# The low-rank gate's panel ahead of the last pair of heads, and its logits inside that pair's last panel

## What is computed

```
q, k, v, qg, kg, vg, glr, rg = split(h @ w_in)          # glr is [T, 16]
o_a = moba_attention(q, k, v, rp_table)                 # 8 heads of 64, here in 4 pairs
log_a = log_sigmoid(glr @ w_gate_up + b_gate) / 16      # the logits
o_g = gla_chunked(qg, kg, vg, log_a)
o_g = rms_norm(o_g, g_norm) * silu(rg)
x = x + concat([o_a, o_g]) @ w_out
```

## Time and profile before

| | us |
| --- | --- |
| median of 3 executions | 1539.41 |
| lowest and highest | 1537.49, 1540.6 |
| the profiled execution | 1537.66 |
| its span, first to last instruction | 1535.9 |
| TensorE busy (98% of the span) | 1502.2 |
| VectorE busy | 881.2 |
| ScalarE busy | 562.6 |

### The profile page before, as it was taken

One profiled execution on the slowest core, in us unless ns is written; L12 is line 12 of the kernel. 1 busy time (PEld: TensorE's weight loads), 2 busy tenths in 40 slices (PEclk: granted clock), 3 DMA queues, 4 the chain that ended last, 5 costly groups with the idle time before them and its releaser, 6 DMA issues.

```text
span 1535.9 us, 20560 instructions
## 1 busy us (share of the span) xinstructions
PE 1502.2 (98%) x7096; PEld 1229.1 (80%) x7096; DVE 881.2 (57%) x1420; ACT 562.6 (37%) x827; POOL 24.4 (2%) x20
## 2 busy tenths in 40 slices
PE   7999999999999999999999999899999999999996
PEld 6877778788888888888888877788888888888885
DVE  6736664675655655434448778955665652255432
ACT  5214544324433333333226545434443321123220
POOL 0000000000000000000000000000000000000000
PEclk9999999999999999999999999999999999999998
DMA  6523222223322222232332231312122322222211
GB/s 238 209 84 96 75 75 89 91 74 105 110 96 96 96 96 96 97 108 96 124 110 83 98 122 55 110 65 73 63 76 83 109 96 93 88 98 99 90 66 55
DMA packets 43014, 148.95 MB, mean 97 GB/s; under 512 B 4632, under 2 KB 5032, under 8 KB 42836
## 3 DMA queue, kind: packets, MB, share of 16 engines
q1 hardware_dynamic: 38688, 137.38, 26.3%
q10 hardware_dynamic: 4276, 10.89, 2.1%
HBM read 146.13 MB, written 6.06 MB: 99 GB/s over the span
## 4 chain that ended last, share of the span: by engine, by line
PE 71%; issue 24%; DVE 4%; ACT 0%; DMA 0%; POOLq 0%; POOL 0%; DVEq 0%; ACTq 0%
PE ps L1078 23%; PE ps L1080 22%; PE ps L1079 22%; PE ps L1208 1%; PE ps L1221 1%; DVE wl L691 1%; DVE a L1843 1%; DVE qe L1830 1%; PE ps L1118 0%; DMA x<-x_dram 0%; PE ps L2182 0%; DVE x L2029 0%; PE ps L1111 0%; DVE msum L1641 0%; DVE hl L703 0%
## 5 line engine op out<-in xcount | busy, mean ns | idle before, releaser
L478 ACT ACTIVATE wh<-stage 128x1024 fp32r<-128x1024 f32 x255 | 270.1, 1059 | 564.2 <-PE ps L1080 563.1
L1078 PE MATMUL ps<-hh,wh 128*128 128x512 f32 x1096 | 436.4, 398 | 10.8 <-DVE hl L703 10.8
L1080 PE MATMUL ps<-hh,wl 128*128 128x512 f32 x1096 | 428.5, 391 | 0.0
L1079 PE MATMUL ps<-hl,wh 128*128 128x512 f32 x1096 | 428.0, 390 | 0.0
L691 DVE TENSOR_TENSOR wl<-stage,wh 128x1024 fp32r<-128x1024 f32 x255 | 311.9, 1224 | 192.8 <-ACT wh L478 192.5
L1078 PEld LDWEIGHTS ps<-hh,wh 128*128 128x128 f32 x1096 | 206.4, 188 | 59.8 <-issue 14.6
L1080 PEld LDWEIGHTS ps<-hh,wl 128*128 128x128 f32 x1096 | 206.3, 188 | 43.7
L1079 PEld LDWEIGHTS ps<-hl,wh 128*128 128x128 f32 x1096 | 206.6, 189 | 39.7
L1080 PE MATMUL ps<-ah,wl 128*128 128x512 f32 x432 | 170.8, 395 | 0.0
L1079 PE MATMUL ps<-al,wh 128*128 128x512 f32 x432 | 170.7, 395 | 0.0
L1078 PE MATMUL ps<-ah,wh 128*128 128x512 f32 x432 | 170.7, 395 | 0.0
(11 more groups left out here) (307 smaller groups left out, 1825.3 us busy)
## 6 DMA issues: line engine op xcount, KB each, us to landing
stage<-stream_dram SPq DMA_DIRECT2D x255, 512.0 KB, 3.2
bias_lines<-bias_line ACTq DMA_DIRECT2D x1, 3840.0 KB
x<-x_dram ACTq DMA_DIRECT2D x4, 512.0 KB, 9.7
bias<-bias_lines ACTq DMA_DIRECT2D x4, 512.0 KB, 5.0
out_dram<-x SPq DMA_DIRECT2D x8, 256.0 KB, 2.1
bias<-bias_lines ACTq DMA_DIRECT2D x4, 256.0 KB, 2.9
mem<-mem_dram ACTq DMA_DIRECT2D x1, 1024.0 KB, 4.8
early<-early_dram SPq DMA_DIRECT2D x1, 512.0 KB, 12.1
```

Of the source, the lines that this page charges most:

```text
L478: A(b.wh[:, p.slot, :], b.stage[:, p.slot, :], ACT.Copy).then_inc(s.hi_ready, 1)
L1078: MM(out, wh, xh, start=start, stop=False, skip_group_check=True)
L1079: MM(out, wh, xl, start=False, stop=False, skip_group_check=True)
L1080: return MM(out, wl, xh, start=False, stop=stop, skip_group_check=True)
```

## The change

The low-rank panel is taken out from behind the last pair and put ahead of it. In the stream of panels it comes between the third and the fourth pair; the last pair's panels are now numbered from P_LAST. Each engine's program follows: TensorE calls `features(Panel(P_GLR), ...)` before `pair_body(3, True)`, VectorE copies its result at the head of the last pair. The two logits' products are made by a new step `logits(r)` inside the last pair's last panel, ahead of its tiles 2 and 6, and go to the banks 4 and 5 instead of 6 and 7. `glr` and `wgu` now lie in `diag` (so rows name them `diag`), and `wgu` is loaded by ScalarE ahead of the pair loop. The three copies of weights and subtractions at the pair's end keep their places and carry other names.

```diff
@@ scalar_program
     pair_parts(0)
+    act.dma_start(b.wgu[0:16, :], dram["wgu"]).then_inc(s.wgu_in, 16)
     hi(Panel(P_VA2 + 3 + RING))
...
     act.dma_start(b.masks[:], dram["late"].rearrange("p (l q) -> p l q", q=P)).then_inc(s.late_in, 16)
-    act.dma_start(b.wgu[0:16, :], dram["wgu"]).then_inc(s.late_in, 16)
-    hi(Panel(P_GLR + RING))
+    hi(Panel(P_LAST + 3 + RING))
     for r in range(2):
         act.wait_ge(s.logit_done, r + 1)
-        A(b.la[:, r, :], b.ps[:, 6 + r, :], ACT.Abs, bias=col(b, "b_gate2", r)).then_inc(s.logit_abs, 1)
+        A(b.la[:, r, :], b.ps[:, 4 + r, :], ACT.Abs, bias=col(b, "b_gate2", r)).then_inc(s.logit_abs, 1)
@@ vector_program, pair_body
+        if last:
+            evac_row(Panel(P_GLR), 0, b.glr, E_GLR % 4)
         dve.wait_ge(s.bias_in, 16 * i + 80)
...
         evac(3)
         if last:
-            lo(Panel(P_PAIRS + 3 + RING, RING, i))
+            lo(Panel(P_LAST + 2 + RING))
@@ behind the pairs
-    dve.wait_ge(s.evac, E_PAIRS + 16)
+    dve.wait_ge(s.evac, E_LAST + 4)
     V.tensor_scalar(b.zg[:, 0:2, :], b.zg[:, 0:2, :], 0.125, None, ALU.mult).then_inc(s.q_scaled, 1)
...
-    evac_row(Panel(P_GLR), 0, b.glr[:], E_GLR % 4)
-    lo(Panel(P_GLR + RING))
+    lo(Panel(P_LAST + 3 + RING))
@@ block2_tensor
+    def logits(r):
+        pe.wait_ge(s.wgu_in, 16)
+        pe.wait_ge(s.evac, E_GLR + 1)
+        if r == 0:
+            pe.wait_ge(s.o_evac, 11)
+        else:
+            pe.wait_ge(s.turned_ready, 48)
+        MM(b.ps[:, 4 + r, :], b.wgu[0:16, P * r:P * r + P], b.glr[0:16, :], start=True,
+           stop=True).then_inc(s.logit_done, 1)
...
+                   {0: [tn(1, 3)], 2: [lambda: logits(0)], 4: [second_values], 6: [lambda: logits(1)]} if last else
                    {0: [tn(1, 3)], 4: [second_values]})
...
     with pe.Fori(0, 3) as i:
         pair_body(i)
-    pair_body(3)
     features(Panel(P_GLR), E_GLR, E_GLR % 4)
-    pe.wait_ge(s.late_in, 32)
-    pe.wait_ge(s.evac, E_GLR + 1)
-    pe.wait_ge(s.turned_ready, 48)
-    pe.wait_ge(s.o_evac, 12)
-    for r in range(2):
-        MM(b.ps[:, 6 + r, :], b.wgu[0:16, P * r:P * r + P], b.glr[0:16, :], start=True,
-           stop=True).then_inc(s.logit_done, 1)
+    pair_body(3, True)
     tokens(P_VG, E_VG, s.v_done)
```

More of the change, by code:

```diff
@@ L48 @@
 P_END1 = P_DOWN + 3 * KT
-(P_QA, P_KA, P_VA2, P_PAIRS, P_GLR, P_VG, P_XV, P_WOUT2, P_XQ, P_XO, P_UP_A, P_DOWN_A, P_UP_B, P_DOWN_B,
- P_END) = (P_END1 + n for n in (0, 4, 8, 12, 28, 29, 33, 41, 49, 57, 65, 81, 97, 113, 129))
+(P_QA, P_KA, P_VA2, P_PAIRS, P_GLR, P_LAST, P_VG, P_XV, P_WOUT2, P_XQ, P_XO, P_UP_A, P_DOWN_A, P_UP_B, P_DOWN_B,
+ P_END) = (P_END1 + n for n in (0, 4, 8, 12, 24, 25, 29, 33, 41, 49, 57, 65, 81, 97, 113, 129))
 E_U, E_VA, E_POOL, E_Q, E_K, E_V, E_GATE, E_PROJ, E_WOUT, E_UP, E_DOWN = 0, 2, 4, 6, 10, 14, 18, 42, 66, 74, 118
 E_END1 = E_DOWN + KT
-(E_QA, E_KA, E_VA2, E_PAIRS, E_GLR, E_VG, E_XV, E_WOUT2, E_XQ, E_XO, E_UP_A, E_DOWN_A, E_UP_B, E_DOWN_B,
- E_END) = (E_END1 + n for n in (0, 4, 8, 12, 28, 29, 33, 37, 45, 53, 61, 77, 85, 101, 109))
+(E_QA, E_KA, E_VA2, E_PAIRS, E_GLR, E_LAST, E_VG, E_XV, E_WOUT2, E_XQ, E_XO, E_UP_A, E_DOWN_A, E_UP_B, E_DOWN_B,
+ E_END) = (E_END1 + n for n in (0, 4, 8, 12, 24, 25, 29, 33, 37, 45, 53, 61, 77, 85, 101, 109))
 M = 256
@@ L220, in semaphores @@
     s.a_cleared, s.ke_cleared, s.q_scaled, s.qk_product = named("a_cleared ke_cleared q_scaled qk_product")
+    (s.wgu_in,) = named("wgu_in")
     (s.xk_hi, s.xk_ready, s.xv_hi, s.xv_ready) = named(
@@ L370, in place @@
     b.vx = at("vx", R(44), [MT, D])
-    b.glr = at("glr", R(52), [T])
-    b.wgu = at("wgu", R(54), [256])
+    b.glr = b.diag[:, 0, :]
+    b.wgu = b.diag[:, 1, 0:256]
     b.yh2 = at("yh2", R(68), [KT, T], F32R)
@@ L1410, in pair_body @@
         act.wait_ge(s.silued, i + 1)
-        act.wait_ge(s.evac, 4 * i + E_PAIRS + 2)
+        act.wait_ge(s.evac, E_LAST + 2 if last else 4 * i + E_PAIRS + 2)
         AR(b.tmp[:, 0, :], b.rg[:, i, :], ACT.Tanh, scale=0.5).then_inc(s.gated, 1)
@@ L1685, in evac @@
         def evac(u):
-            p = Panel(P_PAIRS + u, RING, i)
-            slot = (E_PAIRS + u) % 4
+            p = Panel(P_LAST + u) if last else Panel(P_PAIRS + u, RING, i)
+            slot = ((E_LAST if last else E_PAIRS) + u) % 4
             if u == 0:
@@ L1721, in pair_body @@
         dve.wait_ge(s.gated, i + 25)
-        dve.wait_ge(s.evac, 4 * i + E_PAIRS + 2)
+        dve.wait_ge(s.evac, E_LAST + 2 if last else 4 * i + E_PAIRS + 2)
         V.scalar_tensor_tensor(b.rg[:, i, :], b.tmp[:, 0, :], 1.0, b.rg[:, i, :], ALU.add,
@@ L1744, in block2_vector @@
     st.mark(V.memset(b.reset[:, 0::CHUNK], 0.0))
-    evac_row(Panel(P_GLR), 0, b.glr[:], E_GLR % 4)
-    lo(Panel(P_GLR + RING))
+    lo(Panel(P_LAST + 3 + RING))
     for r in range(2):
         dve.wait_ge(s.logit_abs, r + 1)
-        st.mark(V.tensor_scalar(b.b[:, r, :], b.ps[:, 6 + r, :], col(b, "b_gate2", r), 0.0, ALU.add, ALU.min))
+        st.mark(V.tensor_scalar(b.b[:, r, :], b.ps[:, 4 + r, :], col(b, "b_gate2", r), 0.0, ALU.add, ALU.min))
     q = b.zg[:, 0:2, :].rearrange("p r t -> p (r t)")
@@ L1790, in block2_vector @@
         step()
-    dve.wait_ge(s.late_in, 32)
+    dve.wait_ge(s.late_in, 16)
     dve.wait_ge(s.a_cleared, 2)
@@ L2064, in block2_tensor, with pair_body @@
     pe.wait_ge(s.rowa_ready, 1)
-    def pair_body(i):
+    def logits(r):
[7 more added lines that the diff above has]
+           stop=True).then_inc(s.logit_done, 1)
+    def pair_body(i, last=False):
         def sc(n):
@@ L2096, in pair_body @@
             moving = {} if u < 2 else {"xh": b.memh, "xl": b.meml, "width": M}
-            features(Panel(P_PAIRS + u, RING, i), E_PAIRS + u + RING * i, (E_PAIRS + u) % 4,
-                     between=between[u], **moving)
+            p = Panel(P_LAST + u) if last else Panel(P_PAIRS + u, RING, i)
+            e = E_LAST + u if last else E_PAIRS + u + RING * i
+            features(p, e, (E_LAST + u if last else E_PAIRS + u) % 4, between=between[u], **moving)
     with pe.Fori(0, 3) as i:
         pair_body(i)
-    pair_body(3)
     features(Panel(P_GLR), E_GLR, E_GLR % 4)
-    pe.wait_ge(s.late_in, 32)
-    pe.wait_ge(s.evac, E_GLR + 1)
-    pe.wait_ge(s.turned_ready, 48)
-    pe.wait_ge(s.o_evac, 12)
-    for r in range(2):
-        MM(b.ps[:, 6 + r, :], b.wgu[0:16, P * r:P * r + P], b.glr[0:16, :], start=True,
-           stop=True).then_inc(s.logit_done, 1)
+    pair_body(3, True)
     tokens(P_VG, E_VG, s.v_done)
@@ L2365, in layout @@
     half = FF2 // 2
-    stream += [chunk_panels(w2[:, 0:1024]), row_panels(w2[:, 1024:1536]), pairs, glr,
+    stream += [chunk_panels(w2[:, 0:1024]), row_panels(w2[:, 1024:1536]), pairs[:12], glr, pairs[12:],
                row_panels(w2[:, 2048:2560]), row_panels(xkv[:, D:D + 512]), row_panels(xkv[:, D + 512:2 * D]), chunk_panels(a["w_out_2"][0]),
```

## The result

| | before | changed |
| --- | --- | --- |
| median of 20 executions each, us | 1539.26 | 1541.66 |
| lowest and highest | 1536.01, 1542.52 | 1540.14, 1544.99 |
| ratio of the two (95% interval) | | 1.0017 (1.0011 to 1.0024) |
| profiled execution, its span | 1537.66, 1535.9 | 1540.36, 1538.6 |

The changed kernel is slower by 2.40 us, 0.17%. The interval of the ratio lies wholly above 1, so the difference is clear of the noise.

What follows compares the result with a forecast made beforehand. TensorE, busy 1502.2 of 1535.9 us, was taken as the bound, with VectorE deciding at L2118: -0.77 on TensorE plus 3.2 of standing gave +2.45, so 1540.1 profiled or 1541.9 against the median; range 1538.6 to 1544.3.

Steps and rivals of the forecast that it cites:

- The copy of `glr` leaves the path, hidden at the head of the last pair.: At the old join behind the last pair: the copy's 0.99 us leaves TensorE's path; VectorE's 0.69 for it is covered.
- 1.05 for each insertion, TensorE 0.77 sooner.: Last pair's last panel: two inserted products cost 2.10 us against the join's 2.87, so `vg` starts 0.77 sooner, at 918.11.
- VectorE starts 6.53 later and waits 0.53 for the panel.: VectorE's chain from the last head's values starts at 915.79; its `kx` copy waits 0.53 us for the pair's last panel.
- Net +3.2 at the running sums.: End of VectorE's running sums: delays less removed waits and the copy shift it by +3.2 us, to 933.85.
- 9.42 from the sums to q*k.: VectorE from the running sums' end to the q*k product: 9.64 less a wait of 0.22, done at 943.27.
- TensorE stands for 3.2.: Ahead of the `ones` products (L2118): TensorE, done at 940.13, waits 3.2 us for VectorE's q*k, where before it waited for nothing.
- +2.45 at L2118 and carried 1 to 1.: The `ones` products start at 943.35 instead of 940.90, +2.45 us, and everything behind carries this to the end.
- The gain is kept: Rival: VectorE's chain to q*k is done in time, TensorE does not stand ahead of L2118; 1538.6 us, chance 0.10.
- the point of decision: For the kept gain: q*k must end before 940.13 + 0.1, for which 3.2 us have to leave VectorE's chain.
- The products are dear: Rival: each logits' product inside the panel pays a further break like the join's 0.99; +4.4, 1543.8 us, chance 0.10.
- The clock falls: Rival: the granted clock falls behind TensorE's stand at L2118, costing 1.4 us more; +3.9, 1543.3 us, chance 0.35.

Runs made afterwards that it cites:

- e5: Changed kernel with both logits' products back behind the last pair and the scalings of x spread 3, 2, 3 along VectorE's chain; 1536.98 us, ratio 0.9983.
- e3: Changed kernel with the eight scalings of x moved from ahead of the running sums to behind the chain's three steps; 1537.9 us, ratio 0.999.
- e1: Changed kernel with both logits' products back behind the last pair, the low-rank panel staying ahead of it; 1537.9 us, ratio 0.9994.
- e4: Changed kernel with each logits' product made twice in a row into the same bank; profiled span 1540.4 us.
- e8: Changed kernel with both logits' products together ahead of tile 6 of the last pair's last panel; profiled span 1539.9 us.
- r1: Changed kernel unedited, profiled again on another chip to see its granted clock; 1540.96 us.
- r2: Changed kernel unedited, second repeat on another chip to see its granted clock; 1541.38 us.
- r3: Changed kernel unedited, third repeat on another chip to see its granted clock; 1542.99 us.
- e6: Kernel before, with scalings spread, two level differences and their exponentials made early, a third difference and a subtraction ahead of the states; 1536.64 us, ratio 0.9981.

## Why the prediction was right

The forecast against its own reference was 1537.66 + 2.45 = 1540.1 for a profiled execution; it was 1540.36, of which 0.25 is older than the change. Against the median it was 1541.9; it is 1541.66. That the mechanism held is shown below; that the median agrees to 0.2 us is in part luck, since the forecast had the clock stay up behind the wait, and in three of four profiles of this kernel it did not. Step by step, with the marks taken out:

- **The copy of `glr` leaves the path, hidden at the head of the last pair.** Right. In e5, where VectorE is not late, TensorE is 0.88 earlier for it.
- **1.05 for each insertion, TensorE 0.77 sooner.** The mechanism held, the term was too small. The first product stands between 912.09 and 913.35: 913.35 - 912.21 = 1.14, and the matmul behind it is followed after 0.22 instead of 0.12, another 0.10: 1.24. The row of L1152 had been read up to the next matmul's start and without what that one costs, 0.11 more there; the remaining 0.08 is not explained. Two cost 2.48, not 2.10, against 2.87 for the join: `vg` starts 0.39 sooner (918.49 in before's time, forecast 918.11). In e3 the saving at `ones` is 0.56; 0.11 more is the first `vg` matmul, which no longer follows a plain fp32 product.
- **VectorE starts 6.53 later and waits 0.53 for the panel.** The start is 916.22 - 0.25 = 915.97, forecast 915.79: the first product's 0.19. The wait is 0.76; of the 0.23 above the forecast 0.19 is the second product's. e1 and e4 show that these two terms are real: 1.94 come back with the products behind the pair, 1.71 are added with two more.
- **Net +3.2 at the running sums.** They end at 934.16 - 0.25 = 933.91, forecast 933.85. `kx` starts 0.38 later than forecast (918.94 - 0.25 against 918.31). That is offset because steps in a row overlap at more places than the two I counted: from `kx` to the sums' end it takes 15.22, where the sum had 15.54.
- **9.42 from the sums to q*k.** 943.47 - 934.16 = 9.31. q*k ends at 943.22 in before's time, forecast 943.27.
- **TensorE stands for 3.2.** From 940.51, when the next matmul could have been issued, to 943.52: 3.01. It came 0.13 later than forecast and was released 0.08 sooner.
- **+2.45 at L2118 and carried 1 to 1.** +2.37, and 48.82 against 48.78 in the stretch behind it.

**The rivals.** *The gain is kept* needed a shorter VectorE chain; e3 made it so, and the point of decision was as put: q*k done at 939.84, before TensorE arrives, and no wait. With the scalings where they are it was not to be had. *The products are dear* is refuted: 1.24, not 2.0. *The clock falls* came true in part. It did not in the profile on which the step-by-step reading rests; it did in three of the four profiles of this kernel, by 1.6 to 2.8 us in the stretch and not by the 1.4 that the rival took from the earlier trace rows. That can be more than the whole forecast difference of 2.45, yet the total is the forecast's. In the two of those three profiles that lose 2.8, 1.4 to 1.65 is missing from the loss at the second wait. The rest is in what the median of before contains: its profile (1537.66) is 1.6 below its own median, one step of the last column. So the clock's part of the difference of the medians came out near nothing: 2.40 measured, 2.37 of work. That it cancels here is a reading of thirteen profiles. The runs that were only timed have their mean granted clock on record, to a thousandth, and at the same clock the two kernels lie further apart: at 0.993 the changed kernel has 1541.66 (median of 7), before 1539.63 (12, beside e1 to e4) and 1539.11 (8, beside e5 to e8), 2.0 to 2.6 less; at 0.994 it is 3.7 to 4.0 and at 0.992 2.9 to 3.7, with three to eight executions a side. So the cancelling is rough at best. Had it not cancelled, the rival's 1543.3 would have been the better figure, and its chance should have been put above the forecast's own: the row for it was there, a fall behind 2.07.

The rule cited with this rival, from the Trainium skill, TensorE: Matmul & The Clock Gate, Part 1 (What's actually happening), that the low level is the default and activity releases it, would have the clock low behind the stand. Five profiles agree (0.50 at r1's 944.00), the first of the changed kernel does not (1.00 in the same window).

**What stays open.** What decides whether the clock falls behind the same wait in the same kernel; whether a fall at the first place makes one at the second less likely (it was absent in e4, r1 and r2, present in e8 and r3); and what makes a kernel's share of executions at the lower clock. That share is why the medians of e1 and e3, 1.6 below before, are lower than their starts of `ones` (+0.43 and -0.56) say: eight of e1's ten executions have a mean granted clock of 0.995 or 0.996, three of e3's ten, and two of the 25 of before. At the same clock the order is that of the starts. At 0.993 e3 is 0.7 below before (three against 12) and e1 1.7 above (two against 12); in the other group e5 is 0.7 below at 0.993 and 0.9 at 0.994 (its start of `ones`: -0.88), and e6 2.4 to 2.7 below at 0.992 to 0.994 (its stretch: -2.39).

## What to carry to other kernels

Work on one engine is also cover for what the others do beneath it. Before moving it, list that and ask whether it is late for anything behind; here 5.48 us of a low-rank panel covered the copy of `kx`, a subtraction, a scaling and the clears. An early product delays every chain that forks behind it by its whole time, so, while the other engine is the late one, a small product belongs behind the fork, beside another of its kind. And a difference of 2 us between two profiles is read from a mark ahead of the change to the point where the engines join again: total times here move by steps of 1.6 us with the clock; where each execution has its mean granted clock on record, executions at the same clock can be compared as well.

## What the runs showed of the hardware

- A plain fp32 product with 16 rows and 512 columns costs a stream of fp32r matmuls of 256 columns 1.24 us when it stands alone, 2.10 for two in a row (e8), and 0.86 for a further one behind its like (e4).
- The granted clock fell behind waits of 2.06 and 2.85 us in some profiles of the changed kernel and not in others (0.50 at r1's 944.00, 1.00 in the first profile there). A fall cost 1.6 to 2.8 us behind the first wait and 1.6 or 3.2 (the steps of the last column) from the second on.
- The work up to the point where the engines join repeats to 0.02 us over four profiles of the changed kernel, while the whole span differs by 2.7.
